# Recurrence of an encoder layer: the order inside a unit, with key turnings around the second fill and scores behind the first U, and key loads in front of the blocks

## The reference

```
sa    = state @ kk_t
state = state * w_t - outer(sa, kk_t * a_t) + outer(v_t, k_t)
y_t   = state @ r_t
```

## Time and profile before

| | |
|---|---|
| three timed runs | 1575.39, 1578.98, 1579.17 us, median 1578.98 |
| profiled execution | 1578.85 us, span 1577.1 us |
| TensorE busy over the span | 1467.5 us, 93% |
| VectorE, ScalarE, GpSimd busy | 512.4, 240.7, 179.7 us |
| granted TensorE clock, mean of the span | 0.983 of full |
| units of the recurrence | first fill of unit 0 at 270.1 us, of unit 7 at 507.7 us |

### The profile page before, as it was taken

One profiled execution on the slowest core, in us unless ns is written; L12 is line 12 of the kernel. 1 busy time (PEld: TensorE's weight loads), 2 busy tenths in 40 slices (PEclk: granted clock), 3 DMA queues, 4 the chain that ended last, 5 costly groups with the idle time before them and its releaser, 6 DMA issues.

```text
span 1577.1 us, 25943 instructions
## 1 busy us (share of the span) xinstructions
PE 1467.5 (93%) x11404; PEld 737.5 (47%) x11404; DVE 512.4 (32%) x725; ACT 240.7 (15%) x488; POOL 179.7 (11%) x349
## 2 busy tenths in 40 slices
PE   7999999888897898999999989989989989989996
PEld 6344445888887655434334324324324324324332
DVE  6666634667665555101101101101201201201113
ACT  3334311212221121100000000000000000000002
POOL 1323503433232120000000000000000000000000
PEclk9999999999999999999999999999999999999998
DMA  9245577766755653699999999999999999999995
GB/s 306 67 160 167 181 280 173 157 161 136 144 101 104 247 237 160 241 428 427 428 433 431 426 434 431 427 431 433 431 428 432 435 426 433 433 426 436 420 425 218
DMA packets 172502, 500.46 MB, mean 317 GB/s; under 512 B 125776, under 2 KB 134992, under 8 KB 152960
## 3 DMA queue, kind: packets, MB, share of 16 engines
q1 hardware_dynamic: 166624, 479.30, 78.4%
q0 software_dynamic: 5792, 19.89, 3.7%
HBM read 470.84 MB, written 28.33 MB: 317 GB/s over the span
## 4 chain that ended last, share of the span: by engine, by line
PE 44%; DMA 12%; DVE 2%; issue 1%; ACT 1%; DVEq 0%; SPq 0%
PE pD L1652 13%; PE pU L1622 11%; DMA ring<-in_exp_w_up 10%; PE pG L1622 9%; PE pG L1595 5%; PE pX L1583 4%; DMA ring<-in_exp_w_down 2%; DVE res L1770 1%; DVE hid L1790 1%; PE pX L1633 1%; PE pD L1595 0%; ACT xin L1711 0%; PE pX L1671 0%; DVE res L1808 0%; ACT hidT L1728 0%
## 5 line engine op out<-in xcount | busy, mean ns | idle before, releaser
L1790 DVE TENSOR_TENSOR hid<-silu,pU 128x512 f32<-128x512 f32 x32 | 20.6, 684 | 737.4 <-PE pU L1622 737.4
L1622 PE MATMUL pU<-ring,xin 128*64 128x512 f32 x768 | 177.2, 617 | 26.4 <-DMA ring<-in_exp_w_up 26.4
L1622 PE MATMUL pG<-ring,xin 128*64 128x512 f32 x768 | 169.7, 594 | 6.4 <-DMA ring<-in_exp_w_gate 5.4
L1652 PE MATMUL pD<-ring,hidT 128*64 128x512 f32 x768 | 168.1, 593 | 2.3 <-ACT hidT L1728 2.1
L1622 PEld LDWEIGHTS pU<-ring,xin 128*64 128x64 f32 x768 | 55.9, 142 | 146.0 <-issue 106.8
L1595 PE MATMUL pG<-yexp,scatter 128*128 128x512 f32 x232 | 112.8, 618 | 3.4 <-DVE res L1770 1.9
L1652 PEld LDWEIGHTS pD<-ring,hidT 128*64 128x64 f32 x768 | 55.3, 137 | 108.3 <-issue 106.4
L1622 PEld LDWEIGHTS pG<-ring,xin 128*64 128x64 f32 x768 | 53.6, 137 | 110.2 <-issue 102.0
L1770 DVE TENSOR_TENSOR res<-res,pG 128x512 f32<-128x512 f32 x116 | 78.8, 686 | 43.8 <-PE pG L1595 43.7
L1595 PEld LDWEIGHTS pG<-yexp,scatter 128*128 128x128 f32 x232 | 37.0, 188 | 78.8 <-DVE res L1770 55.1
L1583 PEld LDWEIGHTS pX<-pick,y 128*128 128x128 f32 x512 | 61.0, 199 | 6.6 <-issue 4.2
(11 more groups left out here) (250 smaller groups left out, 1772.2 us busy)
## 6 DMA issues: line engine op xcount, KB each, us to landing
ring<-in_exp_w_down SPq DMA_DIRECT2D x18, 4096.0 KB, 25.8
ring<-in_exp_w_gate SPq DMA_DIRECT2D x18, 4096.0 KB, 31.5
ring<-in_exp_w_up SPq DMA_DIRECT2D x18, 4096.0 KB, 25.1
ring<-in_exp_w_gate SPq DMA_DIRECT2D x12, 2048.0 KB, 24.0
ring<-in_exp_w_up SPq DMA_DIRECT2D x12, 2048.0 KB, 19.2
ring<-in_exp_w_down SPq DMA_DIRECT2D x12, 2048.0 KB, 23.5
lent_slot<-in_exp_w_gate SPq DMA_DIRECT2D x6, 4096.0 KB, 28.7
lent_slot<-in_exp_w_down SPq DMA_DIRECT2D x6, 4096.0 KB, 30.9
```

Of the source, the lines that this page charges most:

```text
L1622: mm = pe.matmul(psum[f // 2][HEAD * s:HEAD * s + HEAD, :], xin[:, k, e, :], w[:, FF * r + HALF * f:FF * r + HALF * f + HALF], start=k == ...
L1652: mm = pe.matmul(pD[h][HEAD * s:HEAD * s + HEAD, :], hidT[:, j, c, HEAD * s:HEAD * s + HEAD], w[:, k, HALF * h:HALF * h + HALF], start=j = ...
L1790: dve.tensor_tensor(hid[:, j, :], silu[:, j, :], pU[j][:, :], ALU.mult).then_inc(hid_done, 1)
```

## The change

On TensorE, the two pairs of key turnings go to the front of the unit: the first behind the first half of N X, the second behind `fill_with_values`. The four groups of scores move forward, the first to right behind `sum_r(1)`, the others behind `sum_y_state(0)`, `sum_y_state(1)` and `solve_u(1)`. The two halves of `cumulate` each stand one block earlier, in front of a `sum_y`. On VectorE, a removed_keys stands behind each half's two additions, `added_keys` around the second pair of `cross`, and the maskings follow the new places of the scores. On SP, `load_keys(n + 3)` stands in front of `blocks(n + 2)`. No instruction is added or dropped.

```diff
@@ -687,10 +687,10 @@
                     load_decays(n + 3)
                     load_queries(n + 3)
                 inverses(n + 1)
+                if n + 3 < UNITS:
+                    load_keys(n + 3)
                 if n + 2 < UNITS:
                     blocks(n + 2)
-                if n + 3 < UNITS:
-                    load_keys(n + 3)
             for a in range(2):
                 sp.wait_ge(base_in[a], 32 * UNITS)
             sp.wait_ge(tk_mm, 4 * LAST)
@@ -974,18 +974,19 @@
                     pe.wait_ge(inv_ev, FILLS * n)
                     pe.wait_ge(r_ev, 2 * n)
                 fill(n, 0, 0, scored(n), of(X))
+                turn_keys(n, (0, 1))
                 pe.wait_ge(v_in[n % 2], V_SUM * (n // 2 + 1))
                 if n:
                     for e in range(2):
                         pe.wait_ge(u_ev[e], 2 * n)
                 fill_with_values(n)
+                turn_keys(n, (2, 3))
                 for g in range(2):
                     pe.wait_ge(inv_ev, FILLS * n + 1 + g)
                     if n:
                         pe.wait_ge(y_ev, 2 * n - 1 + g)
                     fill(n, 2 + g, g, of(XT[n % 2]), of(W))
                     fill(n, g, g, of(W), of(XT[n % 2]))
-                    turn_keys(n, (2 * g, 2 * g + 1))
                 sum_r_state(n, 0)
                 for g in range(2):
                     pe.wait_ge(inv_ev, FILLS * n + 3 + 2 * g)
@@ -997,32 +998,33 @@
                     pe.wait_ge(s_ev, steps_summed(n - 1))
                 solve_u(n, 0)
                 sum_r(n, 1)
+                if ahead:
+                    scores(n + 2, 0)
                 for e in range(2):
                     pe.wait_ge(u_ev[e], 2 * n + 1)
                 pe.wait_ge(tk_ev, 4 * (n + 1))
                 sum_state(n, 0)
                 sum_y_state(n, 0)
+                if ahead:
+                    scores(n + 2, 1)
                 pe.wait_ge(s_ev, steps_summed(n - 1) + 1 if n else 1)
                 sum_r_state(n, 1)
-                if ahead:
-                    scores(n + 2, 0)
                 sum_y_state(n, 1)
                 if ahead:
-                    scores(n + 2, 1)
+                    scores(n + 2, 2)
                 solve_u(n, 1)
                 if ahead:
-                    scores(n + 2, 2)
+                    scores(n + 2, 3)
                 for e in range(2):
                     pe.wait_ge(u_ev[e], 2 * n + 2)
                 if ahead:
                     sum_state(n, 1)
-                    scores(n + 2, 3)
+                if n + 3 < UNITS:
+                    cumulate(n + 3, (0, 1))
                 sum_y(n, 0)
                 if n + 3 < UNITS:
-                    cumulate(n + 3, (0, 1))
+                    cumulate(n + 3, (2, 3))
                 sum_y(n, 1)
-                if n + 3 < UNITS:
-                    cumulate(n + 3, (2, 3))
 
         @block.vector
         def _(dve):
@@ -1129,29 +1131,29 @@
                 for g in range(2):
                     add_to(n, X, g, 2 + g, 3 + 2 * g)
                     add_to(n, XT[n % 2], g, g, 4 + 2 * g)
+                    if ahead:
+                        removed_keys(n + 2, g)
                 if ahead:
-                    removed_keys(n + 2, 0)
+                    added_keys(n + 2, 0)
                 for g in range(2):
                     cross(n, 1, g, 2 + g, 7 + g)
+                if ahead:
+                    added_keys(n + 2, 1)
                 for g in range(2):
                     add_to(n, XT[n % 2], g, g, 9 + g)
-                if ahead:
-                    removed_keys(n + 2, 1)
                 removed(n, 0)
                 if ahead:
-                    added_keys(n + 2, 0)
+                    masked(n + 2, 0)
                 add_state(n, 0)
                 if n == LAST:
                     scale_and_add(dve, keep, 0, v_last)
                 if ahead:
-                    added_keys(n + 2, 1)
-                    masked(n + 2, 0)
                     masked(n + 2, 1)
+                    masked(n + 2, 2)
                 removed(n, 1)
                 if ahead:
-                    masked(n + 2, 2)
+                    masked(n + 2, 3)
                     add_state(n, 1)
-                    masked(n + 2, 3)
                 add_y(n, 0)
                 add_y(n, 1)
                 if ahead:
```

## The result

The changed kernel takes 1595.2 us (median of 4 runs, 1594.35 to 1595.65) against 1577.7 us before (4 runs): ratio 1.0102, 95% interval 1.0081 to 1.0122. It is slower by some 16 us by the ratio (17.5 by the medians), where 6 were forecast and 1592.0 was the end of the range. The profiled execution took 1595.65 us with a span of 1593.9, 16.8 above the one before, so all of it is inside the trace.

A forecast was written before the change was run, and what follows sets the result against it. TensorE's matmul stream was taken to set a unit's length, with VectorE some 10 us to spare. 1578.85 plus 3.3 (9.65 - 5.1 - 0.85 - 0.4) plus 2.6 for the clock gave 1584.8, rounded 1585.0 us; range 1577.5 to 1592.

The forecast's parts named there:

- The turnings were only moved, so TensorE's own work in front of the pair is the same: Before TensorE's last fill pair, at T+11.1: its own work stays unchanged, so it now stands idle for 2.3 us.
- Key loads before blocks: I count 0, bounds -1 and +2 us: On SP, two 512 KB key DMAs, some 1 us of issue, precede the blocks' two: 0, bounds -1 and +2 us.
- Rival (c): Key loads make blocks, base and inverses late, deciding from a delay of 6.0 us: 1590 us; chance 0.06.
- The front of a unit, VectorE: VectorE's longer list up to its last addition delays solve_u's second half in units 0 to 4: +9.65 us.
- The back: Later in units 0 to 4, the moved scores remove score waits and idle time before sum_state: -5.1 us.
- The clock: TensorE's new 2.3 us gap makes the granted clock fall: two falls counted at 1.3 us, +2.6, bounds 0 and 9.6.
- starts: Unit 1's wait for its inverse is covered, -0.85 us; unit 5's last masking comes earlier for unit 7, -0.4 us.
- +3.3 us at an unchanged clock: Over the recurrence: 9.65 - 5.1 - 0.85 - 0.4, before any loss from the clock.
- rival (a): The shift happens without clock loss, TensorE's own stalls falling into the gap: +3.3 down to 0, 1581 us; chance 0.27.
- (b): VectorE finishes the keys by TensorE's last fill pair, T+11.1, so key products cost TensorE nothing: 1572 us; chance 0.12.
- (d): Turnings at unit starts don't count as work, so the clock falls in every unit: 12.8 us more, 1595 us; chance 0.05.

The follow-up runs named there:

- turn0_old_b: The changed kernel with the turnings of unit 0 alone at their old places, repeated on one chip with the others: 1588.88 us, ratio 1.0064.
- two_back_b: The changed kernel with unit 0's turnings at their old places and load_keys behind the blocks: 1584.98 us; as two_back on another chip 1586.72; both ratio 1.0037.
- keys_only: The kernel before with only load_keys(n + 3) moved in front of blocks(n + 2) on SP: 1587.36 us, ratio 1.0045.
- held8: two_back with 8 spare matmul calls on TensorE in front of the last pair of fills in units 0 to 5: 1583.07 us, ratio 1.002.
- keys_early: The changed kernel with unit 0's turnings at their old places and load_keys(n + 3) in front of inverses(n + 1): 1580.86 us, ratio 1.0006.
- turn_only: The kernel before with only the key turnings moved to the front of the unit: 1589.82 us, ratio 1.0057.
- keys_mid: The kernel before with only load_keys(n + 3) moved in front of inverses(n + 1): 1587.62 us, ratio 1.0038.
- clock_held: two_back with 16 spare matmul calls on TensorE in front of the last pair of fills in units 0 to 5: 1586.42 us, ratio 1.0043.

## Why the prediction was wrong

Two steps failed, a wait that was not looked up (some 4.4 us) and a term put at nothing (some 3.9 us), by the differences on one chip, where the change cost 13.7 us. By the prediction's own steps:

- **"The turnings were only moved, so TensorE's own work in front of the pair is the same"** failed in unit 0, by a wait that was added and not looked for: 4.4 us. ScalarE's first copy into TK waits for v's store out of TK, whose buffer `v_stage` shares (`v_out`); that wait ended at 276.6 before too. The row was in the trace: ScalarE's first TK copy began at T+6.5 behind the store's DMA, harmless as long as the third turning stood at T+7.1 and needed it only there; at T+3.2 TensorE stands.
- **"Key loads before blocks: I count 0, bounds -1 and +2 us"** failed: 3.9 us in the change (turn0_old_b less two_back_b), 7 us alone. The step counted SP's issue time and looked at TensorE's waits of before, which is the wrong slack. Rival (c) had the mechanism but reckoned 6 us of slack from the last masking to the unit after next. The slack that decides is that of SP's own loop, one unit long: its waits for masks in the five passes with a load, 19.0 us in four and 3.0 in the fifth. In keys_only the later issue of the blocks (2 us), a later NB (1.0 to 3.1 us) and a longer way from the read of NB to the inverses' write (0.4 to 2.1 us) use that up.
- **The front of a unit, VectorE**: the mechanism was right. No idle time on VectorE from the second mask to cross(1, 0), the pair of fills at T+13.1 for T+13.4, waits of 1.6 to 2.1 us for W in units 1 to 5 for 2.3. What that is worth in time was put too high, as below.
- **The back**: right. One score wait of 0.30 and one of 0.38 are left in a unit, and the idle time before `sum_state` is gone.
- **The clock**: open in its size. It fell in unit 0 behind the wait for TK (granted 0.50 from 278 to 280) and in later units, seven falls for three before; it stands at 0.50 for some 31 us of the recurrence for 14 before. If all of these 17 us were TensorE's to pay, that would be 8 us, half of them (my estimate of the upper bound); the forecast's +2.6 and held8's 1.9 us are less, and no run fixes it.

The sum for front, back, starts and clock was +5.9 us, and two_back, which has that order, measured +5.4 on one chip and +7.8 (5.8 by the ratio) on the other. That it fits is luck in part. The prediction's sum took the late keys as removed, and in two_back they are not. keys_early is the same order with the keys in time, and it measured +1.9 us by the medians, ratio 1.0006 (0.999 to 1.0022): the +3.3 us at an unchanged clock are just inside that interval, the +5.9 us are not. The front's term let TensorE's stalls of before stand in the rest of the unit; in keys_early those without a releaser fell from 11.4 to 4.3 us.

That is rival (a)'s mechanism in its main part, and its time, though the clock fell five times there; for the changed kernel as a whole (a) is out, by the time alone, though its stalls fell to 5.2 us too. (b) is out by the 9.6 us for W. (d) named 1595 us, which is the time that was measured, and is still out: in turn_only the turnings stand at the front of every unit, and the granted clock is 1.00 in units 2 to 4. In the changed kernel a fall begins in unit 1 only at T+13, where the wait for W is, and in unit 3 none begins at all.

The forecast's direction was right and its range 3 us short. The direction, too, hangs on the two steps that failed: with the keys loaded early and unit 0's turnings left where they were, the order by itself shows no cost clear of noise.

## What to carry to other kernels

When work moves forward, look up each of its waits in the first pass of the loop too, where buffers are still lent to the stage before. When a DMA is moved in an in-order queue, follow the queue's whole round trip per pass and compare it with the pass; that the engines show no wait on it says nothing of how much room it has. The engine with 10 us to spare in a unit of 34 had none in the stretch where the work was put: take the room stretch by stretch.

## What the runs showed of the hardware

- The writes of the inverses issued right behind loads of 1 MB on the same queue took 2.7 to 5.5 us to issue in five passes, where 1.3 to 2.1 are usual (keys_mid). The blocks' writes behind the same loads took 1.3 to 1.8 us to issue, but the read that waits for them could go only 6.6 to 7.9 us after they left, for 4.9 to 6.5 before (keys_only).
- 128x128 `matmul` calls in 32-bit floats show as two matmuls each, which start 0.12 us apart (32 from 281.73 to 285.50, clock_held), while transpositions of the same size show as one each and start 0.13 us apart (8 from 274.15 to 275.18, the kernel before).
- The granted clock fell to 0.50 in an idle time of TensorE of 4.6 us (turn_only, unit 0, at 276), behind one of 2.1 us (the changed kernel, unit 1, from 321.9), and not behind one of 2.2 us (the kernel before, unit 6).
